# Two transformer blocks on one core: 26 instead of 24 weight units in the seven-product form, their weight sums by accumulating DMAs, and their operand sums spread over other units

## The reference, cut to what matters

```python
def sqrelu_mlp(hn, w1, w2):
    u = hn @ w1.astype(hn.dtype)
    u = jnp.square(jax.nn.relu(u))
    return u @ w2.astype(hn.dtype)
...
def swiglu(h, w_in, w_out):
    gate, up = jnp.split(h @ w_in, 2, axis=-1)
    return (jax.nn.silu(gate) * up) @ w_out
```

## Time and profile before

| | us |
|---|---|
| median of 3 runs (2065.16 to 2066.45) | 2065.99 |
| the profiled execution | 2061.95 |
| its span, first to last instruction | 2060.2 |
| TensorE's mean granted clock, share of the full one | 0.977 |

### The profile page before, as it was taken

One profiled execution on the slowest core, in us unless ns is written; L12 is line 12 of the kernel. 1 busy time (PEld: TensorE's weight loads), 2 busy tenths in 40 slices (PEclk: granted clock), 3 DMA queues, 4 the chain that ended last, 5 costly groups with the idle time before them and its releaser, 6 DMA issues.

```text
span 2060.2 us, 29219 instructions
## 1 busy us (share of the span) xinstructions
PE 1979.1 (96%) x11930; PEld 1722.2 (84%) x11930; DVE 1215.6 (59%) x1617; ACT 804.2 (39%) x1061; POOL 423.2 (21%) x304
## 2 busy tenths in 40 slices
PE   8999989999999999999999999999997899999996
PEld 6788766778888897999899999998884588888895
DVE  6668756655565654122556555566897456556465
ACT  4448734533232433223343232234435444233232
POOL 2012230202112220012221121211245012031122
PEclk9999999999999998999999999999999899999998
DMA  4223111122232221111122222233131022323231
GB/s 175 104 82 115 62 62 62 62 101 84 102 103 82 102 85 61 62 62 42 62 83 103 83 103 103 83 103 104 61 109 36 21 84 101 102 82 103 102 103 61
DMA packets 27850, 175.06 MB, mean 85 GB/s; under 512 B 4409, under 2 KB 4537, under 8 KB 7762
## 3 DMA queue, kind: packets, MB, share of 16 engines
q1 hardware_dynamic: 25680, 167.32, 23.7%
q0 software_dynamic: 1888, 5.90, 0.9%
q10 hardware_dynamic: 162, 0.10, 0.0%
HBM read 171.19 MB, written 4.78 MB: 85 GB/s over the span
## 4 chain that ended last, share of the span: by engine, by line
PE 72%; issue 13%; DVE 6%; ACT 4%; POOL 4%; DMA 2%; SPq 0%; POOLq 0%; DVEq 0%; ACTq 0%
PE lin L533 50%; PE lin L1832 6%; PE aux L1832 4%; POOL squares L752 2%; ACT w_hi L442 1%; DMA w_raw<-in_weights 1%; PE aux L2633 1%; PE aux L1425 1%; DVE w_lo L449 1%; PE lin L1627 1%; PE lin L1380 1%; POOL w_lo L449 1%; PE lin L2603 1%; PE aux L2617 1%; POOL r_t L2249 1%
## 5 line engine op out<-in xcount | busy, mean ns | idle before, releaser
L533 PE MATMUL lin<-x_hi,w_hi 128*128 128x512 f32 (+1 forms) x1160 | 408.9, 353 | 14.1 <-DVE tmp L628 6.4
L533 PE MATMUL lin<-x_hi,w_lo 128*128 128x512 f32 (+1 forms) x1160 | 407.3, 351 | 0.0
L533 PE MATMUL lin<-x_lo,w_hi 128*128 128x512 f32 (+1 forms) x1160 | 406.9, 351 | 0.0
L533 PE MATMUL lin<-v_hi,w_hi 128*128 128x264 f32 (+1 forms) x1136 | 381.2, 336 | 7.1 <-ACT tmp L1916 4.2
L449 DVE TENSOR_TENSOR w_lo<-w_raw,w_hi 128x2048 fp32r<-128x2048 f32 (+1 forms) x120 | 282.2, 2352 | 170.8 <-ACT w_hi L442 170.3
L533 PE MATMUL lin<-v_hi,w_lo 128*128 128x264 f32 (+1 forms) x1136 | 378.2, 333 | 0.0
L533 PE MATMUL lin<-v_lo,w_hi 128*128 128x264 f32 (+1 forms) x1136 | 377.3, 332 | 0.0
L442 ACT ACTIVATE w_hi<-w_raw 128x2048 fp32r<-128x2048 f32 (+1 forms) x131 | 246.5, 1882 | 207.8 <-PE lin L533 197.4
L533 PEld LDWEIGHTS lin<-x_hi,w_hi 128*128 128x128 f32 x1160 | 219.5, 189 | 49.1 <-DVE tmp L628 7.3
L533 PEld LDWEIGHTS lin<-x_lo,w_hi 128*128 128x128 f32 x1160 | 219.7, 189 | 30.1 <-issue 0.2
L533 PEld LDWEIGHTS lin<-x_hi,w_lo 128*128 128x128 f32 x1160 | 219.8, 189 | 29.8
(11 more groups left out here) (449 smaller groups left out, 3872.0 us busy)
## 6 DMA issues: line engine op xcount, KB each, us to landing
w_raw<-in_weights SPq DMA_DIRECT2D x155, 1024.0 KB, 4.8
rel_by_distance<-rel_by_distance POOLq DMA_DIRECT2D x1, 2599.5 KB, 21.0
rel_bias<-rel_by_distance POOLq DMA_DIRECT2D x8, 264.0 KB, 3.0
h<-in_x_t SPq DMA_DIRECT2D x4, 512.0 KB, 8.0
out_t<-h SPq DMA_DIRECT2D x4, 512.0 KB, 2.8
o_t<-in_mem_t POOLq DMA_DIRECT2D x1, 1024.0 KB, 5.0
cst<-in_consts SPq DMA_DIRECT2D x1, 512.0 KB, 9.6
col<-in_cols ACTq DMA_DIRECT2D x1, 67.0 KB, 5.7
```

The costliest lines, as they stand in the source:

```text
L533: last = nc.tensor.matmul(o, a, b, start=(k % (L.kc // k_banks) == 0 and p == 0), stop=((k + 1) % (L.kc // k_banks) == 0 and p == 2))
```

## The change

The change has five parts.

1. `QUADS` gets unit 3 of `up0a` and of `up1a`: 26 quad units instead of 24.
2. The four POOL instructions for a quad unit's weight sums become five DMAs on POOL's queue. The first copies three blocks of the unit from device memory into `w_sum` and may start when `w_sum` is free, at the same time as the unit's own load. Then `s1` (block 3 from device memory added onto block 0 in `w_raw`) and `s3` (block 1 from device memory onto the first block of `w_sum`), then `s2` (`s1` added onto the second block of `w_sum`) after `s1` has landed, and `s4` (`s2` added onto the third) after `s2`. Since all are additions, signs, the order of blocks in a unit and the DVE sums that read the products change with it, without a change in their number or size.
3. PE's order in a quad unit is p1, p2, p6 instead of p1, p6, p2, and the wait for the operand sums stands ahead of p6 and not ahead of the unit.
4. The operand sums move: in `ff1a` one pair's sums at each of units 0 to 3, its rounding and low part one unit later; in `up0a` and `up1a` the sums at units 0, 1, 1, 2, and the other half at units 1, 2, 2, 2.
5. In `up*` DVE does parts 2 and 3 of `quad_lo` behind the gate of the unit and not ahead of it.

```diff
-         **{f"up{n}{part}": at for n in range(2) for part, at in zip("abc", ((5, 7), (1, 3, 5, 7), (1, 3, 5)))}}
+         **{f"up{n}{part}": at for n in range(2) for part, at in zip("abc", ((3, 5, 7), (1, 3, 5, 7), (1, 3, 5)))}}
...
-        def quad_sum(pool, unit, step):
-
-            q = quad_seq[unit]
-            a11, a12, a22, a21 = (w_block(w_raw, unit, x, x + 1) for x in range(4))
-            s3, s2, s4 = (w_sum[:, x * BLOCK_W:(x + 1) * BLOCK_W] for x in range(3))
-            if step == 0:
-                pool.wait_ge(sem(f"w_loaded{unit % 2}"), 16 * (unit // 2 + 1))
-                if q:
-                    pool.wait_ge(sem("w_lo_ready"), quad_units[q - 1] + 1)
-            else:
-                pool.wait_ge(sem("quad_sum"), 4 * q + step)
-            out_t, x, y, op = ((s3, a21, a11, ALU.subtract), (a21, a21, a22, ALU.add),
-                               (s2, a21, a11, ALU.subtract), (s4, a12, s2, ALU.subtract))[step]
-            nc.gpsimd.tensor_tensor(out_t, x, y, op).then_inc(sem("quad_sum"), 1)
-
         def pool_quad_sums(pool, *names):
+
             for name in names:
                 for t in layer[name].quads:
-                    for step in range(4):
-                        quad_sum(pool, layer[name].unit0 + t, step)
+                    unit = layer[name].unit0 + t
+                    q = quad_seq[unit]
+                    block = [weights[unit][:, x * BLOCK_W:(x + 1) * BLOCK_W] for x in range(4)]
+                    s3, s2, s4 = (w_sum[:, x * BLOCK_W:(x + 1) * BLOCK_W] for x in range(3))
+                    s1 = w_block(w_raw, unit, 0, 1)
+                    if q:
+                        pool.wait_ge(sem("w_lo_ready"), quad_units[q - 1] + 1)
+                    pool.dma_start(w_sum[:, :], weights[unit][:, 0:3 * BLOCK_W]).then_inc(sem("quad_base"), 16)
+                    pool.wait_ge(sem(f"w_loaded{unit % 2}"), 16 * (unit // 2 + 1))
+                    pool.dma_start(s1, block[3], accum_op=ALU.add).then_inc(sem("quad_s1"), 16)
+                    pool.wait_ge(sem("quad_base"), 16 * (q + 1))
+                    pool.dma_start(s3, block[1], accum_op=ALU.add).then_inc(sem("quad_s3"), 16)
+                    pool.wait_ge(sem("quad_s1"), 16 * (q + 1))
+                    pool.dma_start(s2, s1, accum_op=ALU.add).then_inc(sem("quad_s2"), 16)
+                    pool.wait_ge(sem("quad_s2"), 16 * (q + 1))
+                    pool.dma_start(s4, s2, accum_op=ALU.add).then_inc(sem("quad_s4"), 16)
...
                 act.wait_ge(sem(f"w_loaded{unit % 2}"), 16 * (unit // 2 + 1))
+                nc.scalar.activation(w_block(w_hi, unit, 1, 2), w_block(w_raw, unit, 1, 2), ACT.Copy)\
+                    .then_inc(sem("quad_w_hi"), 1)
+            elif part == 1:
+                nc.scalar.activation(w_block(w_hi, unit, 2, 4), w_block(w_raw, unit, 2, 4), ACT.Copy)\
+                    .then_inc(sem("quad_w_hi"), 1)
+            elif part == 2:
+                act.wait_ge(sem("quad_s1"), 16 * (q + 1))
                 nc.scalar.activation(w_block(w_hi, unit, 0, 1), w_block(w_raw, unit, 0, 1), ACT.Copy)\
                     .then_inc(sem("quad_w_hi"), 1)
-            elif part == 1:
-                nc.scalar.activation(w_block(w_hi, unit, 1, 3), w_block(w_raw, unit, 1, 3), ACT.Copy)\
-                    .then_inc(sem("quad_w_hi"), 1)
-            elif part == 2:
-                act.wait_ge(sem("quad_sum"), 4 * q + 2)
-                nc.scalar.activation(w_block(w_hi, unit, 3, 4), w_block(w_raw, unit, 3, 4), ACT.Copy)\
-                    .then_inc(sem("quad_w_hi"), 1)
             else:
-                act.wait_ge(sem("quad_sum"), 4 * q + 4)
+                act.wait_ge(sem("quad_s3"), 16 * (q + 1))
+                act.wait_ge(sem("quad_s4"), 16 * (q + 1))
                 nc.scalar.activation(ws_hi[:, :], w_sum[:, :], ACT.Copy).then_inc(sem("w_hi_ready"), 1)
...
-            a, b = ((0, 1), (1, 3), (3, 4))[part]
+            a, b = ((1, 2), (2, 4), (0, 1))[part]
...
-            nc.vector.tensor_tensor(t1, h_half(N, j, 1), h_half(N, j, 0), ALU.subtract)
+            link(dve, nc.vector.tensor_tensor(t1, h_half(N, j, 1), h_half(N, j, 0), ALU.subtract))
             dve.wait_ge(sem("quad_gained"), N.quads0 + j + 1)
-            link(dve, nc.vector.scalar_tensor_tensor(t3, h_half(N, j, 1), N.gain(j), t3, ALU.mult, ALU.subtract))
-            link(dve, nc.vector.scalar_tensor_tensor(t2, h_half(N, j, 0), N.gain(j), t3, ALU.mult, ALU.subtract))
-            nc.vector.tensor_tensor(t4, t4, t2, ALU.subtract).then_inc(sem("quad_raw"), 1)
+            link(dve, nc.vector.scalar_tensor_tensor(t2, t1, N.gain(j), t3, ALU.mult, ALU.subtract))
+            nc.vector.scalar_tensor_tensor(t3, h_half(N, j, 1), N.gain(j), t3, ALU.mult, ALU.subtract)
+            nc.vector.tensor_tensor(t4, t4, t2, ALU.add).then_inc(sem("quad_raw"), 1)
...
-            return ("p1", "p6", "p2", "p7", "p5") + (("p4", "p3") if L.tile0 % 2 == 0 else ("p3", "p4"))
+            return ("p1", "p2", "p6", "p7", "p5") + (("p4", "p3") if L.tile0 % 2 == 0 else ("p3", "p4"))
...
-            pe.wait_ge(sem("quad_lo"), N.quads0 + 4)
             taken = {L.tile(t % 2, m, t // 2)[0]: L.tile(t % 2, m, t // 2)[1] for m in range(2)}
             for name in quad_order(L):
                 bank, b = QUAD_BANK[name]
+                if name == "p6":
+                    pe.wait_ge(sem("quad_lo"), N.quads0 + 4)
...
-        FF_PAIRS = {1: (0,), 2: (1, 2), 3: (3,)}
-        UP_PAIRS = {1: (0,), 2: (1,), 3: (2,), 4: (3,)}
+        UP_SUMS = {0: (0,), 1: (1, 2), 2: (3,)}
+        UP_PARTS = {1: (0,), 2: (1, 2)}
...
                 else:
                     next_quad_hi(act, L, t, 1)
+                if L.name == "ff1a":
+                    act_quad_gained(act, l_ff, t)
+                    if t:
+                        act_quad_operand(act, l_ff, t - 1)
                 next_quad_hi(act, L, t, 2, 3)
                 if after is not None and t == 0:
                     after()
-                if L.name == "ff1a":
-                    act_quad_norm(act, L, t, FF_PAIRS)
...
+            if L.name == "ff1a":
+                act_quad_operand(act, l_ff, 3)
...
                 next_quad_lo(dve, L, t, 3)
+                if L.name == "ff1a":
+                    if t:
+                        dve_quad_operand(dve, l_ff, t - 1)
+                    dve_quad_sums(dve, l_ff, t)
                 if after is not None and t == 0:
                     after()
-                if L.name == "ff1a":
-                    dve_quad_norm(dve, L, t, FF_PAIRS)
...
                 elif t:
                     high(t - 1)
+                if part_a:
+                    for j in UP_SUMS.get(t, ()):
+                        act_quad_gained(act, N, j)
                 if t in L.quads:
                     act_quad_copy(act, L, t)
                 next_quad_hi(act, L, t, 1)
                 if t - 1 in L.quads:
                     high(t - 1)
+                if part_a:
+                    for j in UP_PARTS.get(t, ()):
+                        act_quad_operand(act, N, j)
                 next_quad_hi(act, L, t, 2, 3)
                 if after is not None and t == 0:
                     after()
-                if L.name[3] == "a":
-                    act_quad_norm(act, L, t, UP_PAIRS)
                 if t not in L.quads:
                     silu(t)
+                if part_a and t == 2:
+                    act_quad_operand(act, N, 3)
...
                     next_quad_lo(dve, L, t, 1)
-                next_quad_lo(dve, L, t, 2, 3)
+                if part_a:
+                    for j in UP_SUMS.get(t, ()):
+                        dve_quad_sums(dve, N, j)
                 if after is not None and t == 0:
                     after()
                 if t in L.quads:
@@ -2393,9 +2400,15 @@
                     dve_quad_second_row(dve, L, t).then_inc(sem(f"lin_taken{slot}"), 1)
                     dve.wait_ge(sem(f"lin_taken{slot}"), before + 1)
                     continue
-                if L.name[3] == "a":
-                    dve_quad_norm(dve, L, t, UP_PAIRS)
+                if part_a and t == 1:
+                    dve_quad_operand(dve, N, 0)
+                elif part_a and t == 2:
+                    dve_quad_operand(dve, N, 1)
                 gate(t)
+                next_quad_lo(dve, L, t, 2, 3)
+                if part_a and t == 2:
+                    dve_quad_operand(dve, N, 2)
+                    dve_quad_operand(dve, N, 3)
...
-    return np.concatenate([block(0, 0), block(1, 0), block(1, 1), block(0, 1)], 1)
+    return np.concatenate([block(0, 1), block(0, 0), block(1, 0), block(1, 1)], 1)
```

More of the change, by code:

```diff
@@ L1864, in dve_quad_mid @@
             dve.wait_ge(sem("quad_top"), quad_seq[unit] + 1)
-            nc.vector.tensor_tensor(tmp[:, 0:2, hf:n], spread_row(tmp[:, 0, 0:hf]), lins[:, 1:3, 0:hf], ALU.add)\
+            nc.vector.tensor_tensor(tmp[:, 0:2, hf:n], spread_row(tmp[:, 0, 0:hf]), lins[:, 1:3, 0:hf], ALU.subtract)\
```

(1 more changed line is left out.)

18 lines of the change are left out of this document (5 added, 13 removed).

## The result

| us | before | after |
|---|---|---|
| median of 4 runs each | 2065.57 (2064.07 to 2066.45) | 2100.54 (2098.83 to 2101.18) |
| the profiled execution, its span | 2061.95, 2060.2 | 2101.18, 2099.4 |

What follows compares the result with a forecast made beforehand. The prediction took PE, busy 96% of the span, as the bound. Its terms, -6.6 - 2.7 - 3.5 + 8.3 = -4.5 us, against a median of 2065.99 gave 2061.5 us; range 2055 to 2079.

Steps and rivals of the forecast that it cites:

- The DMAs for the weight sums cost nothing in the forecast: Quad units: the loop from one w_lo_ready to the next, 10.5 + 3A, is 21.6 us against PE's 21.9 or 21.1; cost 0.
- A: Landing time of one accumulating DMA, three in a row per quad unit: at least 3.0, at most 4.4, taken as 3.7 us.
- the lead: Quad units: behind the gate the last weight part is ready 2.3 us before PE wants it (2.6 with 528 tokens).
- The chain of DMAs becomes the bound: Rival: three landings in a row per quad unit, A over 3.7; at 4.4 about 17 us lost, 2079 us; chance 0.27.
- DVE holds up the DMAs' start: Rival: DMA issues on POOL wait for DVE's two-input SBUF instructions, about 0.7 us each, 2079 us; chance 0.05.
- The waits in `up0a` and `up1a`: Rival: PE's forecast new waits at the first units there stay away, the 8.3 us vanish, 2053 us; chance 0.13.
- slow clock: Rival: new waits in up0a and up1a lower PE's clock once or twice, 2.2 us each, 2064 to 2066; chance 0.12.
- ReLU wait and slow clock in ff1a: ff1a, unit 3: PE's wait for ACT's ReLU goes (4.4 us), with the slow clock behind it (2.2): gain 6.6 us.
- two units more in the seven-product form: up0a and up1a: one ordinary unit each becomes a quad unit, gaining 1.48 + 1.18 = 2.7 us.
- old waits in up0a, up1a: PE's waits for the gate and ahead of quad units go, since pairs are done before unit 3: gain 3.5 us.
- new waits, up1a: unit 0, 1, 2, the rest: up1a: operand sums take three units instead of four, DVE is late, PE waits 1.0, 2.1, 1.1, then 0.4 twice: 5.0 us.
- new waits, up0a: up0a: the same piling of DVE's work, with ordinary units 0.53 us longer and DVE's work 3% more: 3.3 us lost.

Runs made afterwards that it cites:

- the run held until s4: The changed kernel, but the load of the unit behind a quad unit waits until s4 has landed: 2058.43 us (kernel before 2064.45), ratio 0.9965.
- the run with plain copies: The changed kernel with plain copies in place of the four accumulating DMAs, sums left out: 2057.71 us in one execution (kernel before 2064.74).

## Why the prediction was wrong

**The step that failed is "The DMAs for the weight sums cost nothing in the forecast".** Its loop counted one load, the quad unit's own. Within the same 21.9 us SP loads the unit behind it too, and nothing in my sum had that load meet the accumulating DMAs. A by itself was right on the average: 4.1, 3.5 and 3.3 us for s1, s2 and s4 without that load beside them, 10.9 together against my 3 x 3.7 = 11.1. The loop is then about 20 us against my 21.6, since the quad unit's own load lands after 5.0 instead of 7.0. Beside the load s2 takes 8 us, the loop 24.8, and the upper bound of 4.4 for A did not hold, since it let only the DMA's own reads and writes add up. With the meeting taken away by one more wait on SP's loads, the 40.5 us went (the run held until s4).

**The second half of it is the lead.** I had 2.6 us and took it for a reserve against a loop that is too long. It also sets which DMA the load meets. With `w_lo_ready` 4.3 us ahead of PE, s2 goes out 1.6 us before the load; with 2.2 us (1228.37 less 1226.21 in the run held until s4) the load would come 6.4 + 2.2 = 8.6 us behind the quad unit's own (8.7 in the run with plain copies, where PE does not wait either), and s2 is issued at 9.3. Then s2 takes 8 us, the chain ends late, the lead is gone at the next quad unit, and the load comes there at 6.4 us (in all chains from the third of a part on but one, 7.6), still earlier in the chain. The loss feeds itself, until a part of the layer ends: it starts at the second chain of each part and never stops within one. In `ff1` the next load comes 11.1 to 11.7 us behind the quad unit's own, and there is no loss. "That eats a lead ... So nothing shows" was the wrong use of the right number.

**The rivals.** "The chain of DMAs becomes the bound" came true, by another mechanism than mine and at 40.5 us instead of 17: not two reads in a row in every DMA, but one DMA in three that meets a load. "DVE holds up the DMAs' start" fell. 20 of the 26 issues of s2 run beside a DVE instruction with two inputs in SBUF, and all take the same time (minimum, median and maximum); one at 1830.39, wholly within a `w_lo` of 2.29 us, landed after 3.3 us like an undisturbed one:

```profile
L374 POOL DMA_DIRECT2D w_sum<-w_raw x26: 845/867/882, 462.1 to 2022.5; - x26
```

The waits in `up0a` and `up1a` did not stay away, and they brought no slow clock: it is 1.00 from 1033 to 1082 and from 1698 to 1746.

**The other terms held.**

| term | forecast | measured |
|---|---|---|
| ReLU wait and slow clock in ff1a | -6.6 | -7.1 |
| two units more in the seven-product form | -2.7 | -2.7 |
| old waits in up0a, up1a | -3.5 | -3.7 |
| new waits, up1a: unit 0, 1, 2, the rest | 1.0, 2.1, 1.1, 0.8 | 0.8, 1.7, 0.9, 0.7 |
| new waits, up0a | 3.3 | 3.0 |
| weight sums by DMAs | 0 | +40.5 |

Two of the new waits, at units 1 and 2 of `up1a` (PE):

```profile
1710.54 0.47 PE L534 MATMUL lin<-v_hi,w_hi 128*128 128x512 f32 x1 [0.61 <-DVE tmp L2349]
...
1723.37 0.47 PE L534 MATMUL lin<-v_hi,w_hi 128*128 128x512 f32 x1 [1.43 <-DVE tmp L2349]
```

Without the last line of the table the sum is -6.4 us, and the run held until s4 shows 2064.45 - 2058.43 = 6.0 us less.

## What to carry to other kernels

When work goes from an engine to DMAs, draw up all transfers of one period, those that are there already too, and look at which of them run at the same time: an undisturbed landing time is no upper bound. An accumulating DMA held the DMA engines over twice as long here as a copy of its size (24.4 against 10.9 us), so keep large loads off it, by one more wait if need be: the next unit's load was issued 16.8 us behind the quad unit's own in the median, instead of 6.4 to 8.8 from the second chain of a part on, and PE did not wait for it. And where a chain's start hangs on its own end, ask what a small delay does to the next round: here some 2 us of lead, given up on DVE in a place where it seemed free, turned a loss of under 4 us into one of 36.
